# A fetch, a transpose slot and a split copy moved, and filler products added, in a two-block transformer kernel

## The reference

```python
x = first_block(x, c, ...)   # adaptive norm; gating unit, attention and pooling branches; merge; w_out; conv feed-forward
h = concat([meta_tokens, x])                      # 16 + 256 rows
z = rms_norm(h) @ w_in                            # q latent, kv latent, rope key, state input u, gates
attn_out = mla_attention(...) @ w_attn_proj
y = gelu(s5_scan(u, ...))
ssm_out = (y @ w_glu_val) * sigmoid(y @ w_glu_gate)
h = h + (sigmoid(g0) * attn_out + sigmoid(g1) * ssm_out) @ w_out
h = h + (silu(m @ w_ffn_gate) * (m @ w_ffn_up)) @ w_ffn_down      # m = rms_norm(h)
return rms_norm(h)[meta:]
```

## Time and profile before

| | |
|---|---|
| median of 3 executions | 3005.38 us (3004.9 to 3008.43) |
| the profiled execution | 3007.13 us, its span 3005.3 us |
| mean granted clock of TensorE | 0.987 of full |
| TensorE products / weight loads busy | 97% / 85% |
| VectorE, ScalarE, GpSimd busy | 62%, 42%, 11% |

### The profile page before, as it was taken

How to read it: one execution, slowest core, us unless ns; L and a number is a source line. 1 busy time by engine, 2 the same in 40 slices (tenths; PEclk the granted TensorE clock), 3 DMA queues, 4 the chain that set the end, 5 groups by cost and what they waited for, 6 DMA issues and landing times.

```text
span 3005.3 us, 42805 instructions
## 1 busy us (share of the span) xinstructions
PE 2910.9 (97%) x17836; PEld 2539.9 (85%) x17836; DVE 1869.8 (62%) x1904; ACT 1259.8 (42%) x1218; POOL 323.9 (11%) x468
## 2 busy tenths in 40 slices
PE   7999999997999999999899999999999999999998
PEld 3687777876999999888787887877889999999887
DVE  5787777786777776554546456764555555555444
ACT  2334544334444444343423433343444343343443
POOL 1000000000000000000004946620000000000000
PEclk9999999998999999999999999999999999999999
DMA  9977878794666655565546652236555555555564
GB/s 408 352 279 270 301 267 310 282 366 174 249 233 244 239 209 195 202 255 205 196 153 220 211 185 80 79 123 250 208 186 191 190 190 194 195 195 205 204 218 170
DMA packets 110047, 667.32 MB, mean 222 GB/s; under 512 B 23520, under 2 KB 25760, under 8 KB 33632
## 3 DMA queue, kind: packets, MB, share of 16 engines
q1 hardware_dynamic: 101728, 626.96, 57.2%
q0 software_dynamic: 8208, 38.80, 3.5%
HBM read 646.24 MB, written 19.48 MB: 222 GB/s over the span
## 4 chain that ended last, share of the span: by engine, by line
PE 87%; DVE 6%; DMA 2%; ACT 2%; issue 1%; SPq 1%; POOL 0%; DVEq 0%; ACTq 0%; POOLq 0%
PE acc L2202 27%; PE acc L2204 26%; PE acc L2203 26%; DMA ada<-ada_stream 2%; DVE w_lo L1358 2%; PE tp L2255 2%; DVE mod_sum L1414 1%; PE ms L2279 1%; ACT w_hi L847 1%; DMA w_raw<-w_stream 1%; PE acc L2779 0%; SPq L443 0%; PE ms L2202 0%; PE ms L2203 0%; PE ms L2204 0%
## 5 line engine op out<-in xcount | busy, mean ns | idle before, releaser
L1358 DVE TENSOR_TENSOR w_lo<-w_raw,w_hi 128x2048 fp32r<-128x2048 f32 (+1 forms) x484 | 1103.3, 2288 | 715.5 <-ACT w_hi L847 695.5
L847 ACT ACTIVATE w_hi<-w_raw 128x2048 fp32r<-128x2048 f32 (+1 forms) x484 | 918.8, 1908 | 870.1 <-DMA w_raw<-w_stream 867.4
L2202 PE MATMUL acc<-h2T_hi,w_lo 128*128 128x256 f32 x2816 | 779.6, 277 | 7.3 <-issue 7.3
L2203 PE MATMUL acc<-h2T_lo,w_hi 128*128 128x256 f32 x2816 | 778.6, 276 | 0.0
L2204 PE MATMUL acc<-h2T_hi,w_hi 128*128 128x256 f32 x2816 | 778.6, 276 | 0.0
L2202 PEld LDWEIGHTS acc<-h2T_hi,w_lo 128*128 128x128 f32 x2816 | 529.4, 188 | 8.3 <-issue 8.2
L2203 PEld LDWEIGHTS acc<-h2T_lo,w_hi 128*128 128x128 f32 x2816 | 529.5, 188 | 0.1
L2204 PEld LDWEIGHTS acc<-h2T_hi,w_hi 128*128 128x128 f32 x2816 | 529.5, 188 | 0.0
L2202 PE MATMUL acc<-w_hi,hid_lo 128*128 128x512 f32 x704 | 274.6, 390 | 0.9 <-DVE w_lo L1358 0.9
L2204 PE MATMUL acc<-w_hi,hid_hi 128*128 128x512 f32 x704 | 274.0, 389 | 0.0
L2203 PE MATMUL acc<-w_lo,hid_hi 128*128 128x512 f32 x704 | 273.9, 389 | 0.0
(11 more groups left out here) (544 smaller groups left out, 3851.1 us busy)
## 6 DMA issues: line engine op xcount, KB each, us to landing
w_raw<-w_stream SPq DMA_DIRECT2D x484, 1024.0 KB, 4.8
ada<-ada_stream SPq DMA_DIRECT2D x80, 1024.0 KB, 7.2
ada_first<-ada_stream SPq DMA_DIRECT2D x16, 1024.0 KB, 12.0
g_dram<-gates_out SPq DMA_DIRECT2D x12, 512.0 KB, 8.0
gates_in<-g_dram POOLq DMA_DIRECT2D x12, 512.0 KB, 5.7
bias_rows<-b_in POOLq DMA_DIRECT2D x18, 256.0 KB, 7.0
x_res<-x POOLq DMA_DIRECT2D x2, 2048.0 KB, 13.4
x_dram<-x_res POOLq DMA_DIRECT2D x2, 2048.0 KB, 8.8
```

Source lines behind the costliest of these rows:

```text
L847: sc.activation(whi[:, s % 4, :, 0:w], raw[:, s % 4, :, 0:w], ACT.Copy).then_inc(hi_made, 1)
L1358: v.tensor_tensor(wlo[:, s % 4, :, 0:w], raw[:, s % 4, :, 0:w], whi[:, s % 4, :, 0:w].bitcast(F32), ALU.subtract).then_inc(lo_made, 1)
L2202: mm(o, sl, mh, start=start, stop=False, skip_group_check=share)
L2203: mm(o, sh, ml, start=False, stop=False, skip_group_check=share)
```

## The change

Four edits. `keep_busy(n)` issues n plain float32 products of the identity with itself (512 columns) into `ms[0]`; nothing reads the result. Ten stand ahead of the first `cols_chunk` of `w_up`, four ahead of the first chunk of the second block. `mid` is called after the first column tile. The two loads `krw` and `rope` are asked for between the two roots, `rope` after a wait for the fifth `x_new`. `ysT_hi` and `ysT_lo` are made in two halves, with a split behind each half on ScalarE and the two halves ahead of `mix` 1 and `mix` 2 on VectorE; TensorE waits for both.

```diff
             first_root(5)
+            fetch("krw", krw[:], a["w_kr"])
+            pool.wait_ge(sem("x_new"), 5)
+            fetch("krw", rope[:], a["rope"])
             pool.wait_ge(sem("sums"), 6)
...
             root(rx2[:], rx2[:])
-            fetch("krw", krw[:], a["w_kr"])
-            fetch("krw", rope[:], a["rope"])
             pool.wait_ge(sem("x_new"), 8)
...
-            sc.activation(ysT[0][:].rearrange("p j (c t) -> p j c t", t=CH4), ysn[:].rearrange("p j t c -> p j c t"),
-                          ACT.Copy).then_inc(sem("ys_hi"), 1)
-            for _ in range(8):
+            for h in range(2):
+                js = slice(h * KS // 2, (h + 1) * KS // 2)
+                sc.activation(ysT[0][:, js].rearrange("p j (c t) -> p j c t", t=CH4), ysn[:, js].rearrange("p j t c -> p j c t"),
+                              ACT.Copy).then_inc(sem("ys_hi"), 1)
+                split()
+            for _ in range(6):
                 split()
...
-                if n == 1:
-                    dve.wait_ge(sem("ys_hi"), 1)
+                if n in (1, 2):
+                    dve.wait_ge(sem("ys_hi"), n)
+                    js = slice((n - 1) * KS // 2, n * KS // 2)
...
-                        if mid and f == 1:
+                        if mid and f == 0:
                             mid(g)
...
+            def keep_busy(n):
+
+                for _ in range(n):
+                    mm(ms[0][:].rearrange("p (a b) -> p a b", b=P), ident[:], ident[:].unsqueeze(1).to_broadcast([P, 4, P]), start=True, stop=True)
+
+            keep_busy(10)
             cols_chunk(h2T, y1_ahead, y1_mid)
...
+            keep_busy(4)
             rows_chunk(nT, TT, [4] * 4, META, ahead=quarters(x, 4, "x_new"))
...
-            pe.wait_ge(sem("ys_lo"), 1)
+            pe.wait_ge(sem("ys_lo"), 2)
```

More of the change, by code:

```diff
@@ L2079, in _ @@
                 b = bank(n + 1)
-                if n == 1:
-                    dve.wait_ge(sem("ys_hi"), 1)
-                    v.tensor_tensor(ysT[1][:].rearrange("p j (c t) -> p j c t", t=CH4), ysn[:].rearrange("p j t c -> p j c t"),
-                                    ysT[0][:].rearrange("p j (c t) -> p j c t", t=CH4).bitcast(F32),
+                if n in (1, 2):
+                    dve.wait_ge(sem("ys_hi"), n)
+                    js = slice((n - 1) * KS // 2, n * KS // 2)
+                    v.tensor_tensor(ysT[1][:, js].rearrange("p j (c t) -> p j c t", t=CH4), ysn[:, js].rearrange("p j t c -> p j c t"),
+                                    ysT[0][:, js].rearrange("p j (c t) -> p j c t", t=CH4).bitcast(F32),
                                     ALU.subtract).then_inc(sem("ys_lo"), 1)
```

## The result

| | before | after |
|---|---|---|
| median | 3005.38 us, 11 executions (3000.95 to 3025.98) | 2999.91 us, 11 executions (2980.26 to 3010.17) |
| the profiled execution | 3007.13 us | 3002.09 us |
| TensorE's mean granted clock | 0.987 | 0.991 |

The account below looks back on a forecast made before the run. TensorE, busy 97% of the span, bounds the kernel; only its idle and lower-clock time can be won. 0.45 + 3.4 + 0.9 + 7.0 + 5.0 = 16.75 us off 3007.13 gives 2990.4, less 1.75 to the median: 2988.7, range 2982 to 2998.

Parts of the forecast that it names:

- Filler at place 1: Ten unread products before the first `w_up` chunk's transposes keep these at full clock, not the products behind: -0.45 us.
- The bound of +1.3: Worst case for the filler before the first `w_up` chunk: a longer stretch at half clock, 1.3 us lost.
- The earlier transposes: Transposes one column tile earlier in the first `w_up` chunk remove three waits of about 1.2 us: -3.4 us.
- Filler at place 2: Four unread products before the second block's first chunk keep two rounds of transposes at full clock: -0.9 us.
- clock held: Rival, 10%: the filler's effect lasts through the transposes to the products, 1.6 us more at place 1, 0.9 at place 2.
- The rope key: Earlier weight fetch cuts TensorE's wait from 5.23 to 1.0 us and keeps the 48 products at full clock: -7.0 us.
- The early fetch does nothing: Rival, 6%: another load or list holds the rope key, so its 7.0 us becomes 0; 2995.7 us.
- The state result: Halved copies remove TensorE's 3.42 us wait in the attention projection and the half clock behind it: -5.0 us.
- The weight stream is late next: Rival, 15%: waits return in projection and first `w_up` chunk for splits whose weights have not landed; gain 11.9, 2993.6 us.
- The overrun: Rival, 3%: filler ahead of the transposes at both places costs too much per product and ends late; 3022 us.
- outside these places TensorE runs without a stop, and what is won stays won: Beyond the listed idle places TensorE never idles, so time won there is kept to the end.
- The 2 us by which executions differ: Assumed spread between executions, used to widen the range to 2982 to 2998 us.

Follow-up runs that it names:

- e1: The kernel before with only the early fetch of the rope key's weights: median 3001.57 us, ratio 0.9976.
- e4: The kernel before with only both pieces of unread filler products: median 3018.57 us, ratio 1.0011.
- e6: The kernel after with ten further calls of `settle`, one behind each pair of chunks of the first `w_up` loop: median 2999.16 us, ratio 0.9948.
- e10: The kernel after with `settle` moved behind the second chunk and without `even_out`'s unread products and transposes: median 2996.46 us, ratio 0.9934.
- e12: The kernel after with `settle` moved behind one more pair of chunks and without the first ten filler products: median 2988.53 us, ratio 0.9939.
- e5: The kernel after without both pieces of filler: median 2988.93 us, ratio 0.9951.
- e8: The kernel after with `settle` using columns of `rstd` for `ones` and writing into `ms[0]`: median 3001.4 us, ratio 0.9942.
- e2: The kernel before with only the transposes one column tile earlier: median 3001.99 us, ratio 0.9967.
- e7: The kernel after without its call of `settle` in the second chunk: median 3001.94 us, ratio 0.9964.
- e9: The kernel after with `settle` moved from within the second chunk to behind it: median 2985.38 us, ratio 0.9910.
- e11: The kernel after with `settle` moved behind one pair of chunks taken out of the first `w_up` loop: median 2992.32 us, ratio 0.9945.
- e3: The kernel before with only the state result split in two halves: median 3008.13 us, ratio 0.9995.

## Why the prediction was right, and where it was not

**The ratio.** The forecast, 2988.7 against 3005.38, is 0.9944; measured were 0.9949. That agreement is partly luck. Where the change works, the traces show -17.89 against the 16.75 summed. The groups differ by more: lower 3005.2 to 2983.1, upper 3021.8 to 3000.8, some 21 to 22 us. 17.9 of them are in the rows; the other 3 to 4 are open. Stage E (-5.78 in this pair of traces) does not account for them. In before TensorE waited there for a split, and the clock fell (timeline of PE, then a window):

```profile
1634.83 0.80 PE L2202 MATMUL acc<-w_hi,nT_lo 128*128 128x512 f32 x1 [2.82 <-DVE w_lo L1358]
```

```profile
1634.20:1641.00 6.80, 6.17 (x15) 4.82 (x16) 3.92 (x3) 6.28 (x6) 6.03 (x11) 0.50 0.55 218
```

That wait comes and goes with the same code: e1 to e4 have 1.15 to 1.74 us of it, no fall of the clock, and E at 265.3 to 265.9; e6, e10 and e12, whose E is that of after, have 2.55 to 2.96 us, the clock at 0.50 behind it, and E at 268.3 to 268.6. The median of after, 2999.91, lies above the range given, since 7 of its 11 executions drew the slower pace. Of all single-call kernels with at least three of the four edits (after, e5, e8 to e12), 36 of 76 lie in the upper group, of before 46 of 116. Whether that is a difference is not shown.

**Filler at place 1** (-0.45). The transposes came at 0.86 of the clock and took 1.16, and the first product came 5.08 behind them instead of 5.53: the size forecast (5.07 to 5.42 in the seven other traces with this filler). The step that failed is that this stays won. The 0.50 stretch began later, in the wait behind the transposes, and ended later: in after the clock is 0.50 until past 722.7, 11 us behind the first transposes; in before the transposes 9.95 us behind them take 1.04. The bound of +1.3 had this mechanism. But the end is not the filler's doing alone, as windows of e2 (without filler) and then of e7 (with it) show:

```profile
719.00:720.00 1.00, 1.00 (x6) 1.00 (x5) 0.41 (x2) 1.00 (x4) 0.00 (x0) 0.50 0.00 0
720.20:721.20 1.00, 1.00 (x11) 1.00 (x10) 0.88 (x3) 1.00 (x2) 0.00 (x0) 1.00 0.00 0
```

```profile
711.80:718.50 6.70, 3.69 (x17) 3.72 (x18) 3.12 (x9) 1.14 (x3) 0.00 (x0) 0.50 0.00 0
718.60:720.00 1.40, 1.40 (x14) 1.40 (x13) 0.35 (x1) 1.40 (x4) 0.00 (x0) 1.00 0.00 0
```

The first transposes start at 709.22 in e2 and at 709.73 in e7. Nine traces have the new slot and the whole of stage A. Where the clock read 0.50 until 8.5 to 9.1 us behind the first transposes (e5, e7, e12), A is 31.99 to 32.23; where it did until 10.4 to 11.1 (after, e2, e6, e8, e9, e11), A is 32.81 to 33.04. With and without filler stand on both sides: e5 against after and e12 against e11 put the filler 0.7 and 1.05 behind, e2 against after level. That it wins anything for the stage is not shown, nor that it costs anything.

**The earlier transposes** (-3.4). e2 against before -3.6, e5 against e3 -4.2; all three waits went. Right, though the end of the 0.50 stretch moves A by up to 1 us.

**Filler at place 2** (-0.9, the first rival's figure 0.9 more). -1.8 and -2.1: mis-sized, because the clock held through both rounds of transposes to the products. So it did in eight of the nine traces with this filler; in e6 it fell (0.51 over 1466.90 to 1470.30), the second transposes took 1.81, and C is 29.73 instead of 28.28. The *clock held* rival was true here and false at place 1. What the places differ in is the idle time behind the filler: 0.54 and 1.56 us here, 2.29 and 3.92 there; no run varies it by itself. The prediction drew on the Trainium skill (TensorE: Matmul & The Clock Gate, Part 4: PE-mode transpose), where work in transpose mode does not count as TensorE being busy in the same way. At place 2 the clock read 1.00 over 16 transposes with 2.1 us of waits around them, and through to the products: the rule, if it holds for them, cost nothing there. At place 1 the clock fell behind the transposes, which agrees with the rule but does not single it out, since 3.92 us of idle time followed them.

**The rope key** (-7.0). The wait went from 5.23 to 0.69 or 0.72 (forecast 1.0), the 48 products from 8.77 to 6.01 or 6.03 (-2.75, forecast -2.8). The other traces with the late fetch have 7.29 to 8.53 (e2, e3, e4), so these products win 1.3 to 2.8 from one trace to the next. Late next is ScalarE's list, as named. In the profiled execution of after the second load was issued at 1472.00 and landed 3.0 us later, long before 1497.73. *The early fetch does nothing* was false.

**The state result** (-5.0). -5.14 and, alone, -5.08 (e3). A wait of 0.36 on a split is left at 2053.45, and the clock stayed at 1.00. *The weight stream is late next* came true as that 0.36 and, in e5's trace, as the 1.64 at 2023.40.

**The overrun.** 20 filler instructions took 8.74 us (forecast 8.6) and ended 2.29 us ahead of the transposes (forecast 2.3); the price that would have decided it was 2.2 us per product.

**What was not in the working.** The prediction took it that a chain of products, once busy, has one pace. The profiled execution of before has 117.8 ns ahead of line 2520 and 113.3 behind it; no row was read for that, since no idle time stands there. That step, "outside these places TensorE runs without a stop, and what is won stays won", holds in stage B and does not fix the time there. Of the whole trace it is not true: idle times over 0.25 us add up to 81 us in before, and those listed (nine, where the text says seven) to 32; the wait of 2.82 us in E is one of the others. "The 2 us by which executions differ", taken from three executions, was the term of the range that was mis-sized: the two groups lie some 17 apart.

**Open.** The 3 to 4 us by which the groups moved further than the rows say, and the 5.5 us of e5, would need more than one trace per kernel. That in this long stage the pace turns at `settle` is shown by e7 (never without it) and e6 (nine times in nine inside the loop). Over all traces, 5 calls of 5 that came at 113.3 ns left 117.8; of the 17 that came at 117.8, 10 left 113.3 and 7 left 117.8, while the pair at line 2888, in the second `w_up` stage, also came at 117.8 and left 113.3 in 14 of 14. Why the first call of the first stage sometimes leaves 117.8 is not shown: its operands (e8), its place (e9, e11) and the first filler (e12) do not decide it. It shows at once, though: in all 36 calls the first two products behind the pair start 205 to 207 ns apart where 113.3 follows and 200 or 201 where 117.8 does. 6 of 7 in e9 is too few to say that its place is better.

## What to carry to other kernels

Before a median is compared, sort the executions: two groups 16 us apart hid terms of 3 to 7 us that a stage of one trace showed plainly (e3). Then take the same stage from every trace whose code there is the same: E differs by up to 5 us among them, and a pair of traces would have been read as a gain. Count instructions per window in a stretch where the engine is fully busy at full clock; the same count should stand in both traces. Unread filler paid where it ended right ahead of the work that needs the clock (0.5 us here), and nothing was shown to be won where waits of 2.3 and 3.9 us followed it.

## What the runs showed of the hardware

Float32r products of 256 columns with a weight load each run at one of two paces, 113.3 or 117.8 ns from start to start, at the same granted clock of 1.00, and keep it for hundreds of microseconds. A pair of small plain float32 products turns one into the other in both directions (e6), but not every time; a few products of 512 columns leave the slow one (all traces with `even_out`). The pace also turns elsewhere: in the first chunk of after, 24 products from 729.75 come at 117.8 ns and, behind eight transposes, 12 from 736.23 at 113.3. In the second `w_up` stage the pair gave 113.3 ns in every trace, and the stage took 480.7 us in all of them. After an idle time of about 4 us the clock was found at either level, and the longer idle time did not mean the lower clock: at place 2, before had its first transposes at 1.94 us behind 3.96 us of idle time, e1 at 1.11 behind 4.17 and e5 at 1.25 behind 4.07.
